# Two attentions: normalising the output instead of the exponentials

## The reference, cut to what matters

```python
logits = jnp.einsum('bqhd,bqkhd->bhqk', qb, kg).astype(f32) * att_scale
logits = jnp.where(valid, logits, -jnp.inf)
p = jax.nn.softmax(logits, axis=-1).astype(vg.dtype)
return jnp.einsum('bhqk,bqkhd->bqhd', p, vg)
```

```python
p = jnp.exp(scores - m[..., None])
den = jnp.sum(p, axis=-1)
num = jnp.einsum('brhnqk,brhnkd->brhnqd', p, vv.astype(jnp.float32))
...
return (num / den[..., None]).reshape(b, s, ATT_WIDTH)
```

## Time and profile before

| | us |
|---|---|
| median of 3 runs | 2056.57 |
| lowest, highest run | 2053.7, 2062.21 |
| profiled execution, own time | 2057.34 |
| its span in the trace | 2055.3 |
| mean granted clock of PE | 0.953 |
| first attention, first logits to last values product | 847.0 to 928.3 |
| second attention, likewise | 1562.9 to 1607.0 |

### The profile page before, as it was taken

How to read it: one execution, slowest core, us unless ns; L and a number is a source line. 1 busy time by engine, 2 the same in 40 slices (tenths; PEclk the granted TensorE clock), 3 DMA queues, 4 the chain that set the end, 5 groups by cost and what they waited for, 6 DMA issues and landing times.

```text
span 2055.3 us, 26036 instructions
## 1 busy us (share of the span) xinstructions
PE 1930.0 (94%) x9160; PEld 1557.4 (76%) x9160; DVE 841.8 (41%) x1409; ACT 841.3 (41%) x1217; POOL 900.1 (44%) x432
## 2 busy tenths in 40 slices
PE   2878999999999999899999999998999999999997
PEld 1767878888887687557888888875886778888886
DVE  6993232222005589862422220267467233222103
ACT  4455444343214443563543431234435344433221
POOL 6663434444444143393444444333434435444441
PEclk7677999999999799999999999999999999999998
DMA  2003223223322122102323222232320113233231
GB/s 94 23 18 141 100 76 109 100 84 101 102 93 98 52 82 72 52 1 72 99 96 102 96 98 94 90 99 74 132 73 31 62 62 119 86 102 102 92 102 41
DMA packets 51664, 170.70 MB, mean 83 GB/s; under 512 B 6672, under 2 KB 11536, under 8 KB 50960
## 3 DMA queue, kind: packets, MB, share of 16 engines
q1 hardware_dynamic: 50448, 166.59, 24.3%
q10 hardware_dynamic: 1152, 3.26, 0.5%
HBM read 165.37 MB, written 2.10 MB: 81 GB/s over the span
## 4 chain that ended last, share of the span: by engine, by line
PE 74%; DVE 13%; DVEq 4%; POOL 3%; ACT 2%; issue 2%; ACTq 0%; DMA 0%; SPq 0%
PE ps L228 22%; PE ps L230 22%; PE ps L229 22%; POOL pr L1266 3%; DVE convT L2061 2%; PE ps L1420 2%; PE ps L1422 1%; PE ps L1421 1%; DVE score L1667 1%; PE ps L1469 1%; DVE rope_a L1602 1%; DVE h_lo L1066 1%; DVE top L1663 1%; DVEq L616 1%; DVE xT L991 1%
## 5 line engine op out<-in xcount | busy, mean ns | idle before, releaser
L218 POOL TENSOR_TENSOR w_lo<-raw,w_hi 128x1024 fp32r<-128x1024 f32 x296 | 721.7, 2446 | 1028.5 <-ACT w_hi L211 1028.5
L228 PE MATMUL ps<-h_hi,w_hi 128*128 128x512 f32 (+1 forms) x1456 | 573.0, 394 | 8.5 <-DVE h_lo L1066 4.6
L230 PE MATMUL ps<-h_hi,w_lo 128*128 128x512 f32 (+1 forms) x1456 | 569.1, 391 | 0.0
L229 PE MATMUL ps<-h_lo,w_hi 128*128 128x512 f32 (+1 forms) x1456 | 568.9, 391 | 0.0
L211 ACT ACTIVATE w_hi<-raw 128x1024 fp32r<-128x1024 f32 x296 | 311.6, 1057 | 506.0 <-PE ps L230 443.8
L228 PEld LDWEIGHTS ps<-h_hi,w_hi 128*128 128x128 f32 (+1 forms) x1456 | 273.6, 188 | 69.2 <-issue 8.6
L230 PEld LDWEIGHTS ps<-h_hi,w_lo 128*128 128x128 f32 (+1 forms) x1456 | 273.6, 188 | 58.9
L229 PEld LDWEIGHTS ps<-h_lo,w_hi 128*128 128x128 f32 (+1 forms) x1456 | 273.8, 188 | 58.4 <-issue 0.5
L228 PE MATMUL ps<-hid_hi,w_hi 128*128 (+1 forms) x528 | 205.4, 389 | 0.0
L229 PE MATMUL ps<-hid_lo,w_hi 128*128 (+1 forms) x528 | 205.4, 389 | 0.0
L230 PE MATMUL ps<-hid_hi,w_lo 128*128 (+1 forms) x528 | 205.4, 389 | 0.0
(11 more groups left out here) (363 smaller groups left out, 2263.4 us busy)
## 6 DMA issues: line engine op xcount, KB each, us to landing
raw<-in_w_gu SPq DMA_DIRECT2D x132, 512.0 KB, 3.4
raw<-in_w_down SPq DMA_DIRECT2D x66, 512.0 KB, 3.4
raw<-in_w_mix SPq DMA_DIRECT2D x33, 512.0 KB, 3.4
raw<-in_w_dsa SPq DMA_DIRECT2D x29, 512.0 KB, 3.4
raw<-in_w_glu SPq DMA_DIRECT2D x16, 512.0 KB, 3.5
raw<-in_w_out SPq DMA_DIRECT2D x12, 512.0 KB, 3.4
raw<-in_w_o SPq DMA_DIRECT2D x8, 512.0 KB, 3.4
s_x<-in_xs SPq DMA_DIRECT2D x1, 2048.0 KB, 10.1
```

What stands on the lines that cost most here:

```text
L218: pool.tensor_tensor(w_lo[slot][:], raw[slot][:], w_hi[slot][:].bitcast(F32), ALU.subtract)\
L228: pe.matmul(o, wh, ah, start=start, stop=False)
L229: pe.matmul(o, wh, al, start=False, stop=False)
L230: return pe.matmul(o, wl, ah, start=False, stop=stop)
```

## The change

The exponentials are no longer scaled. Each pair gets a sixth turned piece, number 5 (`SPREAD`): PE spreads the reciprocals of the pair's row sums over the two column halves of a bank, so that every row of the values product meets its query's factor. ACT copies this piece to SBUF. DVE multiplies the values product by it into a new SBUF buffer `out`, and POOL makes the high part (a copy to fp32r) and the low part (a subtraction) from `out`. `out` and the sixth piece lie in memory that earlier steps of the phase leave free (`relu` in the first attention, `factors` and `junk` in the second). Bank parity runs over six pieces a pair, ACT copies three of them, and two of the exponentials of ACT's loop move behind its third copy. The values product waits for `o_ready` (DVE's multiplication) where it waited for `o_done`. The order of banks in the first projection changes at its end.

The diff, cut to its core (the removed bodies are `scale` of DVE, `scale_end` and `high` of ACT, `low` of DVE and the scaling loop of POOL, all printed above; semaphores and constructor arguments are left out):

```diff
-        PR_BUFS, PIECES = 6, 5
+        PR_BUFS, PIECES, SPREAD = 6, 6, 5
...
-                return (self.pt_act, 2 * j + k // 2 + 1) if k % 2 else (self.pt_dve, 3 * j + k // 2 + 1)
+                return (self.pt_act if k % 2 else self.pt_dve), 3 * j + k // 2 + 1
...
+            def spread_factors(j):
+
+                n = PIECES * j + SPREAD
+                bank_free(n)
+                pe.wait_ge(a.r_ready, j + 1)
+                for tb in range(TB):
+                    for s in range(2):
+                        col = (2 * j + s) * TB + tb
+                        last = pe.matmul(ps[HD * s:HD * (s + 1), T_BANK + n % 2, tb * P:(tb + 1) * P],
+                                         a.den[:, col:col + 1].broadcast_to([P, HD]), ident, start=True, stop=True)
+                last.then_inc(a.pT_ready, 1)
...
                 if j:
-                    pe.wait_ge(a.o_done, j)
+                    pe.wait_ge(a.o_ready, j)
...
-                pe.wait_ge(*a.probs_ready(j, 0))
+                pe.wait_ge(a.p_ready, j + 1)
                 turn(j, 0)
                 turn(j, 1)
                 if more:
                     logits(j + 2, (0, 1))
-                pe.wait_ge(*a.probs_ready(j, 1))
                 turn(j, 2)
...
                 turn(j, 4)
                 if more:
                     logits(j + 2, (6, 7))
+                spread_factors(j)
                 values(j)
...
@@ attn_scalar
             def turned_out(j, k):
                 if j and k == 1:
                     act.wait_ge(a.pv_done, j)
+                if j and k == SPREAD:
+                    act.wait_ge(a.o_ready, j)
...
-                if j:
-                    high(j - 1)
                 turned_out(j, 1)
                 if more:
                     exps(j + 2, range(0, 2))
-                if j == a.pairs - 2:
-                    scale_end()
                 turned_out(j, 3)
                 if more:
-                    exps(j + 2, range(2, 6))
-            high(a.pairs - 1)
+                    exps(j + 2, range(2, 4))
+                turned_out(j, SPREAD)
+                if more:
+                    exps(j + 2, range(4, 6))
...
@@ attn_gpsimd
+            for j in range(a.pairs):
+                pool.wait_ge(a.o_ready, j + 1)
+                pool.tensor_copy(a.hi[:, j, :], a.out[:])
+                pool.drain()
+                pool.tensor_tensor(a.lo[:, j, :], a.out[:], a.hi[:, j, :].bitcast(F32), ALU.subtract).then_inc(a.o_done, 1)
...
@@ attn_vector
-                        dve.wait_ge(a.pT_ready, PIECES * (j - PR_BUFS // 2 + 1))
+                        dve.wait_ge(a.pT_ready, PIECES * (j - PR_BUFS // 2) + SPREAD)
...
-                last = dve.reciprocal(r, r)
-                if j:
-                    last.then_inc(a.r_ready, 1)
-                else:
-                    dve.drain()
-                    scale(0)
+                dve.reciprocal(r, r).then_inc(a.r_ready, 1)
...
+            def scaled_out(j):
+                dve.wait_ge(a.pv_done, j + 1)
+                dve.wait_ge(*a.piece_out(j, SPREAD))
+                if j:
+                    dve.wait_ge(a.o_done, j)
+                dve.tensor_tensor(a.out[:], ps[:, PV_BANK, :], a.pt[SPREAD][:], ALU.mult).then_inc(a.o_ready, 1)
...
                 if j:
-                    low(j - 1)
+                    scaled_out(j - 1)
...
-            rows_tensor(pe, wo, [(o, None) for o in range(KT) if o != PV_BANK] + [(PV_BANK, (att1.o_done, NH // 2))])
+            rows_tensor(pe, wo, [(o, None) for o in range(5)] + [(6, None), (7, att1.piece_out(NH // 2 - 1, SPREAD)), (PV_BANK, (att1.o_done, NH // 2))])
```

More of the change, by code:

```diff
@@ L1103, in build, with __init__ @@
         class Attention:
-            def __init__(self, name, heads, qT, kT, val, mask, pr, pt, nmax, den, hi, lo):
+            def __init__(self, name, heads, qT, kT, val, mask, pr, pt, out, nmax, den, hi, lo):
                 self.heads, self.qT, self.kT, self.val, self.mask = heads, qT, kT, val, mask
                 self.pairs = heads // 2
-                self.pr, self.pt, self.nmax, self.den, self.hi, self.lo = pr, pt, nmax, den, hi, lo
+                self.pr, self.pt, self.out, self.nmax, self.den, self.hi, self.lo = pr, pt, out, nmax, den, hi, lo
                 self.L_ready = sem(name + "_L_ready")
@@ L1113, in __init__ @@
                 self.r_ready = sem(name + "_r_ready")
-                self.scaled = sem(name + "_scaled")
-                self.scaled0 = sem(name + "_scaled0")
                 self.pT_ready = sem(name + "_pT_ready")
@@ L1119, in __init__ @@
                 self.pv_done = sem(name + "_pv_done")
-                self.o_hi = sem(name + "_o_hi")
+                self.o_ready = sem(name + "_o_ready")
                 self.o_done = sem(name + "_o_done")
@@ L1154, in logits, with bank_free @@
                               start=True, stop=True).then_inc(a.L_ready, 1)
+            def bank_free(n):
+                if n >= 2:
+                    pe.wait_ge(*a.piece_out((n - 2) // PIECES, (n - 2) % PIECES))
+            def spread_factors(j):
[8 more added lines that the diff above has]
+                last.then_inc(a.pT_ready, 1)
             def turn(j, k):
                 n = PIECES * j + k
-                if n >= 2:
-                    pe.wait_ge(*a.piece_out((n - 2) // PIECES, (n - 2) % PIECES))
+                bank_free(n)
                 for m, (s, kb, tb) in enumerate(TURNED[k]):
@@ L1228, in turned_out @@
                 act.activation(a.pt[k][:], ps[:, T_BANK + n % 2, :], ACT.Copy).then_inc(a.pt_act, 1)
[L1230 to L1240, removed]
             exps(0, range(8))
@@ L1281, in masks @@
                                              accum_out=a.nmax[:, n:n + 1]).then_inc(a.masked, 1)
[L1283 to L1289, removed]
             def reciprocals(j):
@@ L1306, in turned_out @@
                 dve.tensor_copy(a.pt[k][:], ps[:, T_BANK + n % 2, :]).then_inc(a.pt_dve, 1)
-            def low(j):
-                dve.wait_ge(a.o_hi, j + 1)
-                dve.tensor_tensor(a.lo[:, j, :], ps[:, PV_BANK, :], a.hi[:, j, :].bitcast(F32), ALU.subtract).then_inc(a.o_done, 1)
+            def scaled_out(j):
[4 more added lines that the diff above has]
+                dve.tensor_tensor(a.out[:], ps[:, PV_BANK, :], a.pt[SPREAD][:], ALU.mult).then_inc(a.o_ready, 1)
             masks(0, range(8))
@@ L1330, in attn_vector @@
                     masks(j + 2, (4, 5, 6, 7))
-            low(a.pairs - 1)
+            scaled_out(a.pairs - 1)
         o6 = [BIGR]
@@ L1364, in build @@
         hsq = at("hsq", [TB, GROUP], rope_off)
+        relu = [at(f"relu{n}", [T], SCR + 8 * KB + 2 * KB * n) for n in range(2)]
         pr = [at(f"pr{n}", [N_P], raw_off + 4 * N_P * n) for n in range(PR_BUFS)]
-        pt = [at(f"pt{n}", [T], raw_off + 4 * N_P * PR_BUFS + 2 * KB * n) for n in range(PIECES)]
-        assert raw_off + 4 * N_P * PR_BUFS + 2 * KB * PIECES <= wi_off
+        pt = [at(f"pt{n}", [T], raw_off + 4 * N_P * PR_BUFS + 2 * KB * n) for n in range(SPREAD)] + [relu[0]]
+        assert raw_off + 4 * N_P * PR_BUFS + 2 * KB * SPREAD <= wi_off
         score = [None] + [at(f"score{n}", [T], SCR + 2 * KB * (1 + n)) for n in range(3)]
-        relu = [at(f"relu{n}", [T], SCR + 8 * KB + 2 * KB * n) for n in range(2)]
         A = {n: sem("dsa_" + n) for n in (
@@ L1375, in build @@
         att1 = Attention("att1", NH, qT, kT, val,
-                         lambda tb, h: const("causal") if tb == 0 else score[tb][:, 0:(tb + 1) * P], pr, pt, nmax, den, h_hi, h_lo)
+                         lambda tb, h: const("causal") if tb == 0 else score[tb][:, 0:(tb + 1) * P], pr, pt, relu[1], nmax, den, h_hi, h_lo)
         QI, REM, Q0, Q1, K0, K1, V0, V1 = range(8)
@@ L1753, in build @@
             "y_std", "y_done", "yT_ready", "l_hi")}
-        att2 = Attention("att2", AH, q2T, k2T, v2, lambda tb, h: abias[:, h, (TB - 1 - tb) * P:T], pr2, pt2, nmax2, den2, mix_hi, mix_lo)
+        att2 = Attention("att2", AH, q2T, k2T, v2, lambda tb, h: abias[:, h, (TB - 1 - tb) * P:T], pr2, pt2 + [junk], factors, nmax2, den2, mix_hi, mix_lo)
         n_mix = FIRST["mix"]
```

## The result

The changed kernel takes 2061.86 us (median of 20 runs, 2057.51 to 2070.65); the kernel before, run beside it, 2056.97 us (20 runs, 2051.66 to 2064.34). The ratio is 1.0028, interval [1.0015, 1.0042]: 4.9 us slower (about 3 to 9), clear of the noise and within 0.5%. The forecast was +7.7.

The account below looks back on a forecast made before the run. POOL's scaling was taken as the bound, with PE next at 8.25 us a pair. Removals -6.5, spreading +10.6 and end +3.6 sum to +7.7 us, 2056.57 to 2064.3; own range +4 to +11, 8 in 10 2059 to 2072.

Parts of the forecast that it names:

- (a) four middle pairs: First attention: without scaling, four middle pairs go from 8.50 to 8.25 us each, -1.0 us in all.
- (b) pair 1: First attention: without scaling, pair 1 goes from 8.94 to 8.25 us, -0.7 us.
- (c) two pairs without later logits: Pair 6 of the first attention and its match in the second no longer wait for POOL, -0.6 us each.
- (d) start of the first attention: PE's first transposes no longer wait for DVE's scaling of pair 0; -2.1 us, bounds 1.0 and 2.5.
- (d) start of the second: Same DVE scaling of pair 0 gone, with PE slower there; -1.5 us, bounds 0.5 and 2.5.
- spreading, 12 pairs: Eight added fp32 matmuls on PE in each pair, 0.88 us a pair, nothing hiding them; +10.6 us.
- end of the second, wait: After the second attention PE waits for POOL's last low part; +1.9 us, range 1.4 to 2.5.
- end of the second, half clock: After that idle, PE's granted clock falls to half for some 3.3 us; 1.7 us lost.
- Rival 1: All pairs: spreading is hidden in PE's slack, S near 0, the change wins, 2052 to 2054 us; chance 0.07.
- rival 3: Spreading matmuls: the two column halves do not overlap, 1.95 us a pair, +20.5 us, 2077 us; chance 0.09.
- rival 2: Spreading has its own shape change and waits, 1.02 to 1.2 us a pair, 2066 to 2068 us; chance 0.15.
- Rival 4: A new wait of DVE or ACT ends last in each pair, 0.5 us or more, +14, 2070 us; chance 0.07.

Follow-up runs that it names:

- b_no_scale: The kernel before with every multiplication by the reciprocals left out and nothing put in its place; 2046.32 us, ratio 0.9941.
- after_again: The changed kernel run and profiled once more, unchanged; 2065.05 us, ratio 1.0037.
- a_start: The changed kernel with DVE's scaling of pair 0 put back as a multiplication by 1.0, PE waiting for it; 2072.17 us, ratio 1.0065.
- a_late: Against a_both, DVE widens the next pair's reciprocals at the end of its work for a pair, where it is idle; 2054.52 us, ratio 0.9994.
- a_two_spread: The changed kernel with only two of each pair's eight spreading matmuls, all waits kept; 2054.55 us, ratio 0.9990.
- a_transposed: The changed kernel with DVE widening the reciprocals and four PE transposes a pair instead of eight spreading matmuls; 2061.31 us, ratio 1.0008.
- a_tail: The changed kernel with the transpose that waits for POOL put last after the second attention; 2058.62 us, ratio 1.0002.
- a_both: The changed kernel with the edits of a_transposed and a_tail together; 2060.49 us, ratio 1.0006.

## Why the prediction was right

It was right in sign and mechanism; in size it was too high, 4.9 us measured in a forecast range of +4 to +11. By its own steps (negative is gain; measured from the table: what goes by before to b_no_scale, what comes by b_no_scale to after):

| step | predicted | measured |
|---|---|---|
| (a) four middle pairs | -1.0 | -1.00 |
| (b) pair 1 | -0.7 | -0.69 |
| (c) two pairs without later logits | -1.2 | -1.48 |
| (d) start of the first attention | -2.1 | -2.23 |
| (d) start of the second | -1.5 | -3.05 |
| spreading, 12 pairs | +10.6 | +10.3 |
| end of the second, wait | +1.9 | +1.4 |
| end of the second, half clock | +1.7 | +1.6 |
| sum | +7.7 | +4.8 |

The measured sum takes in -0.06 for the values at the end of the first attention. The half clock is the 1.01 above and 0.62 in the first three matmuls of the projection, which take 1.40 us in after (1620.25 to 1621.65) and 0.78 in before. The 4.8 stands beside the 4.9 of the medians; made with after_again's profile in place of after's it is 5.6. That both lie so near to 4.9 is partly luck, since the interval of the runs is 3 to 9.

*POOL is the bound, but PE stands only 0.25 us behind it.* Right. The reading of PE busy 8.25 of 8.25 in one pair where POOL was not yet late is b_no_scale's middle pair. Whoever read the chain alone would have set up to 67 us against POOL; all of the scaling was worth 8.4.

*The spreading, 0.88 a pair.* Right, from the earlier trace rows: 0.91 in pair 0, 0.87 in a middle pair, 0.81 in a last one. The values do not pay for the change of shape twice, they are even 0.06 us shorter. The rule of the Trainium skill weighed there (TensorEngine Tiling (Array Packing), Key Properties: a change of mode drains, the tiles of one mode work in parallel) agrees with these numbers. Rival 1 falls, since PE was idle for nothing in the middle pairs, and rival 3 with it, since eight matmuls at 1.95 would have made a pair of 10.2. Of rival 2 nothing was seen: its 1.02 would have been 9.27 a pair. Rival 4 falls by the windows, where DVE and ACT are at 6.0 and 6.2 of 9.12.

*The start of the second attention* is the term that was mis-sized: -1.5 taken, bound -2.5, -3.05 measured. I counted DVE's 2.46 us as time that PE, slow there, would give back only in part. It gave back nearly all or more: in after_again the start is 19.79, so there the gain is 21.02 - (19.79 - 0.92) = 2.15, and a_start, with 1.98 us of products put back, is 1.81 longer than after_again and 2.71 longer than after. The rest goes together with the stretch of half clock in that start, nine windows in before, six in after_again, three in after and two in b_no_scale. The term is 2.1 to 3.1, by execution, and what decides within that is open.

*The last pairs* gained 0.14 more each than I took: the reciprocal that pair 6 keeps does not lie in PE's way, and pair 7, read as 5.98 from its window, is 5.90 between the starts of its values and those of pair 6.

*The end.* The wait was 2.28, forecast 2.8: POOL's copy took 0.61 us, not the 1.05 between my bounds. The rule of the Trainium skill's GPSIMD Engine Reference, Engine selection, that one-input work runs there at about line rate, was nearer (0.6, and +3.2 for the end; measured +3.0). The half clock came in after, with 1.6 us where 1.7 was taken, and in after_again; a_start shows that it need not, so this term was in part a matter of the execution.

## What to carry to other kernels

When one engine owns the whole chain of a pipelined loop, its removal is worth the distance to the next engine, and one iteration where the owner is not yet late shows it. Work that is moved to the next engine in line costs its full length in each iteration, however little it looks beside the engine that was relieved; here twelve times 0.87 us ate all of a gain of 8.4. Where work is put on an engine with room, look at what the other engines do at that moment: 0.5 us of copies, put between copies that PE waits for and beside POOL's subtraction, took 1.56 and made a last pair 0.65 us longer than in after and 1.1 longer than in a_late.

## What the runs showed of the hardware beside that

- After the same idle of PE at the end of the second attention, 2.28 and 2.29 us, the granted clock fell to 0.50 in after and stayed at 1.00 in a_start. It fell in after_again, a_two_spread and a_transposed too, so in four profiles of five. After 1.42 us (a_tail, a_both, a_late) it stayed up. The same code's start of the second attention took 18.89, 19.79 and 19.89 us (after, after_again, a_tail), with three, six and six full windows of 1 us at 0.50. So a stretch with many waits of PE has a scatter of 1 us that no edit made, and a single profile of each kernel does not resolve less there; the pairs, which agree within 0.01, do.
- POOL's conversion of 128x512 from fp32 took 0.61 us, its subtraction 1.26; the scaling of the same size by a factor of each row had taken 1.57.
- Two DVE copies of 128x256 from a broadcast source took 0.48 to 0.49 us and, beside POOL's subtraction, 1.55 to 1.56.
